# Peer block of a two-block transformer on Trainium2: ScalarE gates the one-hots, VectorE compares four tokens at once, gathered dots move from the choice to the build

## The reference, cut to what matters

```python
q = (xt @ w_query).reshape(T, 8, 2, 128)
s = einsum('thpd,pkd->thpk', q, sub_keys)
s_top, i_top = top_k(s, 16)
cand = s_top[:, :, 0, :, None] + s_top[:, :, 1, None, :]
best, pos = top_k(cand, 16)              # 16 of 16384 experts, per token and head
g = softmax(best)
a = gelu(einsum('thkd,td->thk', expert_u[ib], xb))
out = einsum('thk,thkd->td', g * a, expert_v[ib])
```

## Time and profile before

| | us |
|---|---|
| median of 3 runs | 2851.71 (2849.28 to 2854.62) |
| the profiled execution | 2840.86 |
| its span, first to last instruction | 2838.7 |
| TensorE busy | 2677.1 (94%) |
| VectorE busy | 2188.9 (77%) |
| ScalarE busy | 1005.3 (35%) |
| POOL busy | 403.5 (14%) |
| mean granted TensorE clock | 0.968 |

### The profile page before, as it was taken

The page is one execution under the profiler, slowest core; times in us unless marked ns, Lnnn a source line. Parts: engine busy times, 40 slices in busy tenths (PEclk is TensorE's granted clock), DMA queues, the critical chain, the costliest instruction groups (busy, mean ns, idle before and its releaser), DMA issues.

```text
span 2838.7 us, 39161 instructions
## 1 busy us (share of the span) xinstructions
PE 2677.1 (94%) x13815; PEld 2335.5 (82%) x13815; DVE 2188.9 (77%) x3756; ACT 1005.3 (35%) x1333; POOL 403.5 (14%) x307
## 2 busy tenths in 40 slices
PE   7958989998999999999999997999999998999998
PEld 6753568988999999999999994788877864788886
DVE  6756849988999976688888878778887476587786
ACT  3501533433444433333333322222237555322222
POOL 0011000023222234243333330000000001000000
PEclk9968989999999999999999998999999998999999
DMA  7441012357788799999999981222222200222231
GB/s 271 160 149 45 34 62 75 116 204 265 277 309 296 297 351 363 326 349 347 353 343 343 350 325 60 75 89 103 96 89 104 105 16 1 72 99 89 89 105 65
DMA packets 161341, 515.56 MB, mean 182 GB/s; under 512 B 12000, under 2 KB 77920, under 8 KB 131680
## 3 DMA queue, kind: packets, MB, share of 16 engines
q1 hardware_dynamic: 107536, 309.84, 30.7%
q0 software_dynamic: 41472, 151.01, 14.8%
q10 hardware_dynamic: 12240, 53.48, 4.8%
HBM read 461.86 MB, written 52.43 MB: 181 GB/s over the span
## 4 chain that ended last, share of the span: by engine, by line
PE 74%; DVE 13%; DMA 3%; issue 2%; ACT 1%; DVEq 0%; SPq 0%; ACTq 0%
PE ps L389 21%; PE ps L393 21%; PE ps L392 21%; PE ps L2186 3%; DVE sb_wL L359 2%; PE ps L2399 1%; PE ps L2389 1%; PE ps L2114 1%; DMA sb_rows<-u_rows,sb_row_at 1%; DMA sb_rows<-v_rows,sb_row_at 1%; DMA sb_stage<-v_l 1%; DVE sb_rows L1408 1%; DVE sb_topi L1381 1%; DVE sb_topi L1378 1%; DVE sb_sc_m L1379 1%
## 5 line engine op out<-in xcount | busy, mean ns | idle before, releaser
L389 PE MATMUL ps<-sb_hL,sb_wH 128*128 128x512 f32 (+1 forms) x2240 | 832.4, 372 | 25.5 <-DVE sb_wL L359 18.8
L393 PE MATMUL ps<-sb_hH,sb_wH 128*128 128x512 f32 (+1 forms) x2240 | 822.2, 367 | 0.0
L392 PE MATMUL ps<-sb_hH,sb_wL 128*128 128x512 f32 (+1 forms) x2240 | 821.7, 367 | 0.0
L359 DVE TENSOR_TENSOR sb_wL<-sb_stage,sb_wH 128x2048 fp32r<-128x2048 f32 (+2 forms) x256 | 537.9, 2103 | 215.5 <-ACT sb_wH L354 214.7
L354 ACT ACTIVATE sb_wH<-sb_stage 128x2048 fp32r<-128x2048 f32 (+2 forms) x256 | 445.5, 1758 | 318.2 <-PE ps L389 176.7
L389 PEld LDWEIGHTS ps<-sb_hL,sb_wH 128*128 128x128 f32 x2240 | 424.7, 190 | 79.9 <-DVE sb_wL L359 20.7
L392 PEld LDWEIGHTS ps<-sb_hH,sb_wL 128*128 128x128 f32 x2240 | 424.8, 190 | 49.3 <-issue 1.2
L393 PEld LDWEIGHTS ps<-sb_hH,sb_wH 128*128 128x128 f32 x2240 | 424.1, 189 | 49.7
L389 PE MATMUL ps<-sb_waL,sb_wH 128*128 128x384 f32 x1024 | 346.3, 338 | 8.2 <-DVE sb_waL L1556 8.2
L392 PE MATMUL ps<-sb_waH,sb_wL 128*128 128x384 f32 x1024 | 345.1, 337 | 0.0
L393 PE MATMUL ps<-sb_waH,sb_wH 128*128 128x384 f32 x1024 | 345.0, 337 | 0.0
(11 more groups left out here) (368 smaller groups left out, 3358.8 us busy)
## 6 DMA issues: line engine op xcount, KB each, us to landing
sb_stage<-u_l SPq DMA_DIRECT2D x64, 1024.0 KB, 7.1
sb_stage<-v_l SPq DMA_DIRECT2D x64, 1024.0 KB, 7.0
sb_stage<-up_l SPq DMA_DIRECT2D x44, 1024.0 KB, 4.8
g_scratch<-sb_ga ACTq DMA_DIRECT2D x64, 384.0 KB, 6.3
w_scratch<-sb_wst ACTq DMA_DIRECT2D x12, 2048.0 KB, 9.4
sb_wg<-w_scratch SPq DMA_DIRECT2D x32, 768.0 KB, 6.2
sb_scr<-g_scratch SPq DMA_DIRECT2D x64, 384.0 KB, 4.5
sb_stage<-down_l SPq DMA_DIRECT2D x44, 512.0 KB, 3.2
```

Of the source, the lines that this page charges most:

```text
L359: dve.tensor_tensor(wL[k % SLOTS][:, 0:n], stage[k % STAGES][:, 0:n], wH[k % SLOTS][:, 0:n], ALU.subtract).then_inc(w_split, 1)
L389: m = pe.matmul(dst, lh, rl, start=first, stop=False)
L392: pe.matmul(dst, ll, rh, start=False, stop=False)
L393: return pe.matmul(dst, lh, rh, start=False, stop=last)
```

## The change

The constants: no dots in the choice, and three a step in the whole build. VectorE compares four tokens in one instruction for both one-hots, without the gate. ScalarE multiplies `oneI` by the gate in place, four activations of 128x128 a group, each with a column of `fromsel` as its scale; its copy of a group's product moves behind the gating of the next group. TensorE's spread waits for both compares and for the gating.

```diff
@@ -76,7 +76,7 @@
 
 W_FIRST = 20
 W_END = W_FIRST + TD // 16
-ROUNDS_A, ROUNDS_B, ROUNDS_W, ROUNDS_C, ROUNDS_L, ROUNDS_V = 20, 12, 8, 12, 8, ROUNDS // 16
+ROUNDS_A, ROUNDS_B, ROUNDS_W, ROUNDS_C, ROUNDS_L, ROUNDS_V = 0, 12, 12, 12, 8, ROUNDS // 16
 FIRST_C = ROUNDS_A + ROUNDS_B + ROUNDS_W * ((W_END - W_FIRST) // 4 - 1)
 assert FIRST_C + ROUNDS_C * ((PEER_STEPS - W_END) // 4 - 1) + ROUNDS_L == ROUNDS
 D_ORDER = (4, 5, 6, 7, 0, 1, 2, 3)
@@ -312,7 +312,7 @@
         s_wo = sems("wout", "proj", "added")
         s_q = sems("query", "keys", "proj", "copied", "scores", "scopied", "top", "negbest", "gexp", "chosen",
                    "trans", "tcopied")
-        s_w = sems("wbuild", "hits", "prod", "copied", "st0", "st1")
+        s_w = sems("wbuild", "hits", "gated", "prod", "copied", "st0", "st1")
         s_u = sems("units", "a", "gelu", "st0", "st1")
         s_g = sems("rows", "tok", "copied", "at", "ld0", "ld1", "ld2", "ld3", "used", "gelu", "out")
         def row_landed(r, i=0, per=0):
@@ -843,6 +843,15 @@
                     act.wait_ge(s_w["copied"], g0 + 1 + 16 * i)
                     act.dma_start(wd[g0 // (TB // 4) + 2 * i], wst[par][:, :, :]).then_inc(s_w[f"st{par}"], 16)
 
+            def gate_hits(g0, i=0):
+
+                act.wait_ge(s_w["hits"], 2 * g0 + 1 + 32 * i)
+                one = oneI[g0 % 4]
+                for t in range(4):
+                    op = act.activation(one[:, t, :], one[:, t, :], ACT.Copy,
+                                        scale=fromsel[:, 2, bass.ds(4 * g0 + t + 64 * i, 1)])
+                op.then_inc(s_w["gated"], 1)
+
             for s in range(W_FIRST):
                 split_hi(act, C_PEER + s + 2)
                 for tt in range(1, TT):
@@ -863,7 +872,11 @@
                     for m in range(2):
                         unit_gelu(W_FIRST + q, m, i)
                         for g in range(2):
-                            spread_copy(4 * q + 2 * m + g, i)
+                            gate_hits(4 * q + 2 * m + g, i)
+                            if 4 * q + 2 * m + g >= 1:
+                                spread_copy(4 * q + 2 * m + g - 1, i)
+                            if 4 * q + 2 * m + g == 15:
+                                spread_copy(15, i)
                     unit_store(W_FIRST + q, i)
             with act.Fori(0, (PEER_STEPS - W_END) // 4 - 1) as i:
                 for q in range(4):
@@ -1415,12 +1428,6 @@
                 dve.scalar_tensor_tensor(tok[:, :], rows[r % 4][:, :], column(row_act, r, i, per), tok[:, :],
                                          ALU.mult, ALU.add).then_inc(s_g["used"], 1)
 
-            def early_dots(tt, j):
-
-                n = 4 * (tt - 2) + j
-                for r in range(ROUNDS_A * n // 8, ROUNDS_A * (n + 1) // 8) if tt >= 2 else ():
-                    row_dot(r)
-
             def row_places():
 
                 for g in range(SLOT_GROUPS):
@@ -1449,7 +1456,6 @@
                                   v[:, :, 0, 1:8].unsqueeze(3).broadcast_to([P, PEER_H, 7, 8]),
                                   v[:, :, 1, 0:8].unsqueeze(2).broadcast_to([P, PEER_H, 7, 8]), ALU.add)
                 split_lo(dve, C_PEER + 2 + 4 * tt)
-                early_dots(tt, 0)
                 chain(dve.tensor_tensor(cand[:, :, 72:80], v[:, :, 0, 8:16],
                                         v[:, :, 1, 0:1].broadcast_to([P, PEER_H, 8]), ALU.add))
                 top16([(cand[:, h, :], cand2[:, h, :], best[:, h, :], pos[:, h, :]) for h in range(PEER_H)])
@@ -1475,7 +1481,6 @@
                 if tt == 1:
                     row_places()
                 split_lo(dve, C_PEER + 3 + 4 * tt)
-                early_dots(tt, 1)
                 keyed = topk[:, tt, :, :].rearrange("p (h two) a -> p h two a", two=2)
                 for half in range(2):
                     dve.tensor_tensor(picks[half].rearrange("p (h k) a -> p h k a", h=PEER_H),
@@ -1484,7 +1489,6 @@
                                       ALU.bitwise_xor).then_inc(v_chain, 1)
                 chain.n += 2
                 split_lo(dve, C_PEER + 4 + 4 * tt)
-                early_dots(tt, 2)
                 dve.wait_ge(v_chain, chain.n)
                 dve.wait_ge(s_q["gexp"], tt + 1)
                 chain(dve.tensor_reduce(gsum[:, 0, :], best[:, :, :], AX, ALU.add))
@@ -1495,7 +1499,6 @@
                                   gsum[:, 1, :].unsqueeze(2).broadcast_to([P, PEER_H, TOPK]),
                                   ALU.mult).then_inc(s_q["chosen"], 1)
                 split_lo(dve, C_PEER + 5 + 4 * tt)
-                early_dots(tt, 3)
                 dve.wait_ge(s_q["chosen"], 3 * tt + 1)
             key_indices(TT - 1)
 
@@ -1512,12 +1515,8 @@
                     dve.wait_ge(s_w["prod"], g0 - 3 + 16 * i)
                 def picked(r):
                     return fromsel[:, r, bass.ds(4 * g0 + 64 * i, 4)].unsqueeze(2).broadcast_to([P, 4, P])
-                dve.tensor_tensor(oneJ[par], iota4, picked(1), ALU.is_equal)
-                for t in range(4):
-                    at = bass.ds(4 * g0 + t + 64 * i, 1)
-                    op = dve.tensor_scalar(oneI[par][:, t, :], tab[:, IOTA, :], fromsel[:, 0, at], fromsel[:, 2, at],
-                                           ALU.is_equal, ALU.mult)
-                op.then_inc(s_w["hits"], 1)
+                dve.tensor_tensor(oneI[par], iota4, picked(0), ALU.is_equal).then_inc(s_w["hits"], 1)
+                dve.tensor_tensor(oneJ[par], iota4, picked(1), ALU.is_equal).then_inc(s_w["hits"], 1)
 
             for q in range(4):
                 for g in range(4):
@@ -2179,7 +2178,8 @@
                 pe.transpose(ps[:, 4 + r, 0:P], chosen[:, r, :], tab[:, IDENT, :]).then_inc(s_q["trans"], 1)
 
             def spread_four(g0, i=0, first=False):
-                pe.wait_ge(s_w["hits"], g0 + 1 + 16 * i)
+                pe.wait_ge(s_w["hits"], 2 * g0 + 2 + 32 * i)
+                pe.wait_ge(s_w["gated"], g0 + 1 + 16 * i)
                 if not first:
                     pe.wait_ge(s_w["copied"], g0 - 3 + 16 * i)
                 for q in range(4):
```

## The result

| | before | changed |
|---|---|---|
| median, us (4 runs each, side by side) | 2850.49 (2847.65 to 2854.62) | 3016.82 (3010.96 to 3025.91) |
| ratio | | 1.059 (95%: 1.0568 to 1.0611) |
| profiled execution; its span | 2840.86; 2838.7 | 3025.91; 3023.8 |
| TensorE / VectorE / ScalarE busy | 2677.1 / 2188.9 / 1005.3 | 2763.4 / 2150.5 / 1107.3 |
| mean granted clock | 0.968 | 0.949 |

The change costs 166 us between the medians; the forecast was 155 (3006). VectorE got lighter by 38 us and ScalarE heavier by 102, and neither number says much, as neither engine bounds the build: the place to look is TensorE's waits there.

The account below looks back on a forecast made before the run. TensorE was taken to bound the kernel, full in the build, with time to win in the choice alone. Gate waits 137 plus clock 35 less gain 17 made 155 us slower, 3006 us on the median's scale, range 2940 to 3065.

Parts of the forecast that it names:

- Gate waits: Build: TensorE's spread waits for ScalarE's gates queued behind the gelu, 2.76 us a half step, 137 us lost with store issues.
- first wait of a half: Build: TensorE's wait before a half step's first spread group, for gelu and four gates, 1.90 us.
- bound on the gate: Build, ScalarE: gates start 0.16 us apart at the cheap bound, 0.40 at the dear one; 0.29 was taken.
- How the waits split: Build, each half step: first wait 1.90 us, second 0.76, dearer first matmuls 0.1, together 2.76.
- Clock: Build: about every second half followed by 3.2 us at clock 0.50; 35 us lost, bounds 0 and 77.
- Choice: Choice: moving its 20 dots out shortens TensorE's waits and slow matmuls, 17 us gained, bounds 12 and 20.
- Dots in the build at no cost: Build: three dots a step instead of two fit VectorE, 10.5 us of work with cheaper compares; cost zero.
- (a): Rival, build: the clock never falls, +120 us, 2972; chance 0.16.
- (b): Rival, build: the clock is down for a stretch in each half, +197 us, 3049; chance 0.10.
- (c): Rival, build: gates at the cheap bound, 0.16 us apart, +70 us, 2922; chance 0.09.
- (d): Rival, build: gates are out of the way in time, only the choice's gain counts, faster at 2835; chance 0.04.
- (e): Rival, choice: its gain isn't there, as the build takes over a backlog, +170 us, 3022; chance 0.60 together with the forecast.

Follow-up runs that it names:

- e5: Changed kernel plus filler matmuls of constant tables ahead of TensorE's gate waits, eight and three a half step: 2969.01 us, ratio 1.0424 to the kernel before.
- e1: Changed kernel with a half's gates ahead of its gelu, ScalarE's chunk split behind the first two gatings: 2862.91 us, ratio 1.0043 to the kernel before.
- e2: Kernel before with only the dots moved out of the choice, three a build step, old compares and gating kept: 2841.73 us, ratio 0.9972.
- e4: Changed kernel without any gating, and without TensorE's wait for it: 2832.01 us, ratio 0.9938 to the kernel before.
- e6: Changed kernel with two gating activations a group instead of four: 2915.03 us, ratio 1.0229 to the kernel before.
- e7: e1 with VectorE's chunk split behind all four compares of a step instead of the first two: 2832.63 us, ratio 0.9938 to the kernel before.
- e9: Changed kernel with both groups' gates straight behind the gelu and both copies behind them: 2978.6 us, ratio 1.0462 to the kernel before.
- e3: Changed kernel with the dots back where they were before, partly in the choice, new gating kept: 3034.97 us, ratio 1.0653 to the kernel before.

## Why the prediction was right

It forecast +155 us by gate waits of 137, a clock loss of 35 and a gain of 17. Measured, the three are 135, 48 and 18, which give the 166 of the medians within a microsecond. Term by term:

**Gate waits: right, to 2 us.** The forecast was 137 at full clock. e5 holds the clock at 1.00 and its build is 135 us longer. A gate was put at 0.39 us and 0.29 from start to start: 0.391 median, eight in 2.43. The first wait of a half was put at 1.90, and is 1.74 to 1.93 (once 2.79). The half step was put at 8.7, and is 8.72 to 8.82 in the 15 halves at full clock, and in nearly all of e5. Neither bound on the gate came true: the address takes 46 ns on ScalarE's sequencer, and with it the gates still start 0.29 apart.

**How the waits split: the sum right, the parts not.** An ordinary half was to have 2.66 us of idle time and 0.1 of dearer matmuls. TensorE's time line of the changed kernel, two ordinary halves, the spread's groups alone:

```profile
849.63 1.16 PE L2186 MATMUL ps<-sb_scr 128*128 128x128 f32 x8 [1.74 <-ACT sb_scr L851]
...
851.28 1.16 PE L2186 MATMUL ps<-sb_scr 128*128 128x128 f32 x8 [0.49 <-ACT sb_scr L851]
...
981.62 1.16 PE L2186 MATMUL ps<-sb_scr 128*128 128x128 f32 x8 [1.74 <-ACT sb_scr L851]
...
983.27 2.08 PE L2186 MATMUL ps<-sb_scr 128*128 128x128 f32 x8 [0.49 <-ACT sb_scr L851]
```

The second group starts 1.65 us behind the first, as forecast (1.66). But a group of eight behind a wait shows as 1.16 us, where 16 without one took 1.95, so it is busier and the idle before it shorter: 2.23 idle and 0.53 more busy are the same 2.76. That is why the build's idle time is 111 us and not 128 to 132, and why 25 (48 x 0.53) of the 76.8 us of added busy time aren't the clock's.

**Clock: mis-sized.** "24 x 1.6 = 38; I take 35 us". e5 measures 48. The mechanism was the one named; the pair of halves above shows it, with 1.16 us for the second group at full clock and 2.08 at the lower level. And the plain halves come out as taken, in part by luck: 26 of 41 are slow, 10.1 us on the average, so 1.3 over the 8.75, 35 us together, where 24 of 48 at 1.6 were forecast (and 35 taken for 38 without a reason). What the sum lacks is the clock behind the stores, for which I had put in the issue alone, 4 us in all. The time line of the changed kernel in such a half:

```profile
753.07 1.13 PE L2186 MATMUL ps<-sb_scr 128*128 128x128 f32 x8 [1.87 <-issue]
...
753.61 0.34 ACTq L844 DMA_DIRECT2D w_scratch<-sb_wst  x1
754.16 1.28 ACT L851 ACTIVATE sb_scr<-sb_scr,sb_fromsel 128x128 f32<-128x128 f32 x4 [0.72 <-ACT sb_wst L839]
...
755.54 1.19 PE L2186 MATMUL ps<-sb_scr 128*128 128x128 f32 x4 [1.35 <-DVE sb_scr L1518]
```

The second gap is 1.35 and not 0.49, 0.86 more for copy and issue where I had 0.6. But in all six halves of this kind the clock then falls, and for longer. The windows behind it (changed kernel):

```profile
755.50:757.60 2.10, 2.06 (x9) 2.09 (x10) 0.44 (x1) 0.43 (x1) 1.59 (x2) 0.50 0.90 374
757.60:763.50 5.90, 5.90 (x24) 5.58 (x23) 1.29 (x2) 0.00 (x0) 0.00 (x0) 0.69 1.02 351
```

A store half costs 12.2 - 8.75 = 3.4 us and not 0.6. With the clock held (e5) it is 9.55, so the issue costs 0.8 and the clock 2.6; six of them make some 16 us. Taken from the half steps' lengths the clock's loss is thus 35 + 16 = 51 us, and 48 by e5's median; 35 were forecast, and the stores' part is what was missing. It is also what makes the build 474 us long where 420 to 460 were to be seen.

**Choice: right, and 1.3 us short in the profile.** The first spread was forecast near 707 and stands at 712.19, of which 1.93 is its own first wait for the gates and 1.4 a delay that this execution carried before the choice (553.79 and 555.21 at the same matmul). The tiles end at 710.26 instead of 724.53, 14.3 + 1.4 = 15.7 us gained of 17. The waits at 672 and 703 are gone, as predicted. The one at 627 was forecast to be 3.6 and is 5.59 in this profile, with the slow clock behind it:

```profile
628.61 0.69 PE L389 MATMUL ps<-sb_hL,sb_wH 128*128 128x384 f32 x1 [5.59 <-DVE sb_wL L359]
```

(changed kernel, time line of TensorE). Here the load of chunk 10 came later than before (VectorE's split at 608.49, has 605.15; 1.4 us of the difference is the delay named above). In the seven experiments whose choice holds no dots and whose gathers stand where they did (e1, e2, e4, e5, e6, e7 and e9) it is 2.6 to 3.9 us. Behind it the clock stays up in e1, e6, e7 and e9; in e2, e4 and e5 it falls some 1.5 us later, for about ten matmuls (e2, time line of TensorE):

```profile
625.65 0.44 PE L389 MATMUL ps<-sb_hL,sb_wH 128*128 128x384 f32 x1 [3.86 <-DVE sb_wL L359]
...
627.23 0.52 PE L393 MATMUL ps<-sb_hH,sb_wH 128*128 128x384 f32 x1
```

So whether a wait of 3.6 us leaves the clock up, which the prediction left open at 2.8 us, has no single answer; where it didn't, ten matmuls at 0.15 more cost 1.5 us. By the medians, e3 less the changed kernel, the gain is 18 us.

**Dots in the build at no cost: right.** e7's build is full with three dots a step. e2 shows where that comes from: with the old compares they cost 5 us.

**Rivals.** (a), the clock never falls, gave 2972, which is e5's 2969; what it lacked was the clock. (b), the clock down in each half, gave 3049: too much, as 15 of 47 are at full clock. The Trainium skill, TensorE: Matmul & The Clock Gate, section "A second HAM failure mode: psum-queue depth-cycling", has the clock swing when TensorE idles for short times between groups of matmuls. The runs agree that it swings, with 48 us lost, but it did so in two halves of three, and in e6, with 1.3 us of waiting in 7.5, only once. (c) falls, for the gate is 0.29 apart. (d) needed ScalarE to take a gate before the gelu; e1 and e7 do just that, and e7's 2832.6 is (d)'s 2835. (e) falls, as e2, e4 and e3 less the changed kernel all show a gain from the choice. (Its loss adds up to 172, 137 + 35, and not 170.)

## What to carry to other kernels

When an engine gets new work whose result the bounding engine waits for, look at what stands ahead of it in its own queue, and whether that waits for the bounding engine: eight gates of 0.29 us cost nothing ahead of the gelu (e7), and behind it some 2.8 us a half step and the clock on top. Place such work ahead of everything that depends on the tile in progress, then follow the chain once more, since a second circle may stand behind the first (e1). Where an order can't be mended and the clock falls behind short gaps, filler matmuls in the gaps can hold it: here they gave back 48 of 166 us.

## What the runs showed of the hardware that I had not expected

- Single gaps in the choice left the granted clock up in four executions (2.63, 2.67, 3.02 and 3.26 us, in e7, e1, e6 and e9; every matmul behind them takes 0.34 again after a first of 0.44 or 0.45). In three others (3.04, 3.73 and 3.86 us, in e4, e5 and e2) the matmuls behind the gap ran at full pace for some 1.5 us, and then about ten took 0.52. Behind gaps of 5.59 us or more the very first was slow (0.69, then 0.52). And a pair of gaps of 1.74 and 0.49 us within a half step of 8.7 lowered the clock in most halves of the changed kernel. A gap of 3.04 lowered it where one of 3.26 didn't, so length alone doesn't decide. What does stays open.
- The halves of the changed kernel aren't alike, though their gaps are: in the one to three behind a store half, which had run slow, the clock stays up, and then it falls again in three to six. In e3, whose gates are the same, the pattern is regular from the first such store on: three halves of 8.7 to 8.8 us, four of 9.7 to 10.3, and the store's of 12.2. With the copies moved (e9) the pattern is irregular, and 21 of 48 are slow. No run here isolates the reason.
- Matmuls behind a wait show as longer without the clock: eight of a group take 1.16 us behind a gap of 0.49 or 1.74, and 16 in a row 1.95. An idle time read from the trace therefore understates what a wait costs, here 2.23 us for 2.76; the distance from one half step to the next doesn't.
